# Five re-orderings in a two-block transformer kernel: first loads, one mean, block sums, a final scaling, and spatial gating in two halves

## The reference, cut to what matters

```python
# first block, x is [1, 1024, 1024]
h = rms_norm(x, mix_norm_g);  p = h @ w_in
y_a = spatial_gating(gelu(gm_u), gelu(gm_v), ...)   # layer norm of v, 4 causal 128x128 mixes, times u
y_b = conformer_conv(cv_a, cv_g, ...)               # 31-tap depthwise convolution, layer norm, silu
y_c = gated_deltanet(q, k, v, gate, beta, alpha, ...)
x = x + concat(y_a, y_b, y_c) @ w_out
h = rms_norm(x, ffn_norm_g)
x = x + (silu(h @ w_gate) * (h @ w_up)) @ w_down    # "ffn0"
x = rms_norm(x, final_norm_g)
# second block, 16 meta tokens put in front
x = x + 0.5 * swiglu(rms_norm(x, ...))              # "ffn1"
x = x + (attention and state-space branches) @ w_out_2   # "mix2"
x = x + 0.5 * swiglu(rms_norm(x, ...))              # "ffn2"
return rms_norm(x, final_norm_2)[:, 16:]
```

## Time and profile before

| | |
|---|---|
| median of 3 runs | 3499.8 us (3498.15 to 3500.18) |
| the profiled execution, its own time | 3500.61 us |
| its span, first to last instruction | 3498.8 us |
| PE busy | 3394.3 us, 97% |
| DVE, ACT, POOL busy | 1870.0, 1086.6, 1312.4 us |
| mean granted TensorE clock | 0.987 |
| the chain that ended last | nearly all PE |

### The profile page before, as it was taken

How to read it: one execution, slowest core, us unless ns; L and a number is a source line. 1 busy time by engine, 2 the same in 40 slices (tenths; PEclk the granted TensorE clock), 3 DMA queues, 4 the chain that set the end, 5 groups by cost and what they waited for, 6 DMA issues and landing times. The chain is left out here.

```text
span 3498.8 us, 52579 instructions
## 1 busy us (share of the span) xinstructions
PE 3394.3 (97%) x19644; PEld 2852.8 (82%) x19644; DVE 1870.0 (53%) x3044; ACT 1086.6 (31%) x1960; POOL 1312.4 (38%) x1559
## 2 busy tenths in 40 slices
PE   7999889999999999999999999999999999999998
PEld 5788778788888889899999878887778878888886
DVE  6966456766552263322221473846877476656324
ACT  5344533323321142111111243215664333332112
POOL 4433035455543352223322442311014545555334
PEclk9999899999999999999999999999999999999999
DMA  3112123332334321111111232101015333231543
GB/s 120 49 43 64 33 80 119 129 109 98 131 124 173 113 84 44 47 39 50 52 41 53 85 111 83 37 24 48 31 40 187 97 121 133 98 132 67 194 170 111
DMA packets 110227, 311.76 MB, mean 89 GB/s; under 512 B 21456, under 2 KB 24656, under 8 KB 109008
## 3 DMA queue, kind: packets, MB, share of 16 engines
q1 hardware_dynamic: 79344, 219.88, 19.5%
q10 hardware_dynamic: 30688, 89.22, 6.8%
HBM read 242.27 MB, written 65.73 MB: 88 GB/s over the span
## 5 line engine op out<-in xcount | busy, mean ns | idle before, releaser
L766 POOL TENSOR_TENSOR w_lo<-w_raw,w_hi 128x256 fp32r<-128x256 f32 (+4 forms) x1288 | 918.9, 745 | 1729.1 <-ACT w_hi L722 1728.8
L931 PE MATMUL acc<-h_hi,w_hi 128*128 128x512 f32 (+1 forms) x2576 | 927.3, 360 | 23.9 <-POOL w_lo L766 10.3
L932 PE MATMUL acc<-h_lo,w_hi 128*128 128x512 f32 (+1 forms) x2576 | 919.4, 357 | 0.0
L933 PE MATMUL acc<-h_hi,w_lo 128*128 128x512 f32 (+1 forms) x2576 | 918.4, 357 | 0.0
L931 PEld LDWEIGHTS acc<-h_hi,w_hi 128*128 128x128 f32 x2576 | 487.2, 189 | 99.0 <-issue 22.6
L932 PEld LDWEIGHTS acc<-h_lo,w_hi 128*128 128x128 f32 x2576 | 487.4, 189 | 69.5 <-issue 1.9
L933 PEld LDWEIGHTS acc<-h_hi,w_lo 128*128 128x128 f32 x2576 | 486.9, 189 | 69.8
L722 ACT CAST w_hi<-w_raw 128x1024 fp32r<-128x1024 f32 (+4 forms) x322 | 275.9, 858 | 831.4 <-PE acc L933 760.9
L749 POOL TENSOR_TENSOR w_lo<-w_sum,w_hi 128x512 fp32r<-128x512 f32 x180 | 264.5, 1474 | 276.1 <-ACT w_hi L1303 276.1
L931 PE MATMUL acc<-ff_hi,w_hi 128*128 128x512 f32 (+1 forms) x960 | 341.8, 356 | 8.5 <-POOL w_lo L766 3.9
L932 PE MATMUL acc<-ff_lo,w_hi 128*128 128x512 f32 (+1 forms) x960 | 337.7, 352 | 0.0
(11 more groups left out here) (435 smaller groups left out, 5172.8 us busy)
## 6 DMA issues: line engine op xcount, KB each, us to landing
w_raw<-in_w_in_dram SPq DMA_DIRECT2D x60, 512.0 KB, 3.6
w_raw<-in_ffn_w_dram SPq DMA_DIRECT2D x58, 512.0 KB, 3.6
ff_kept<-ff_hi SPq DMA_DIRECT2D x36, 512.0 KB, 7.6
ff_kept<-ff_lo SPq DMA_DIRECT2D x36, 512.0 KB, 8.3
w_raw<-in_ffn_w_dram SPq DMA_DIRECT2D x18, 1024.0 KB, 5.6
w_raw<-in_w_out_dram SPq DMA_DIRECT2D x32, 512.0 KB, 3.5
x<-x_kept ACTq DMA_DIRECT2D x6, 2080.0 KB, 8.1
w_raw<-in_w_gate_dram SPq DMA_DIRECT2D x9, 1024.0 KB, 6.3
```

Source lines behind the costliest of these rows:

```text
L766: pool.tensor_tensor(w_lo[:, j, a:a + step], w_raw[:, j, a:a + step], w_hi[:, j, a:a + step].bitcast(F32), ALU.subtract).then_inc(split_do ...
L931: pe.matmul(bank, wh, rh, start=(k == 0), stop=False)
L932: pe.matmul(bank, wh, rl, start=False, stop=False)
L933: ins = pe.matmul(bank, wl, rh, start=False, stop=(k == seg.kt - 1))
```

## The change

Five things are re-ordered. No arithmetic is added or dropped.

1. Start: parts 4 and 5 of x go from ACT's queue to SP's, behind a wait for part 1 and ahead of `consts`; `w_hi` of the first two slabs is made after the second and sixth row.
2. `pe_early`: the second half's mean is formed after four of the eight k of the first slab.
3. Sevens: the sums are formed in the order `FORMED`, with s6 and s7 ahead of s1 and s3; ACT's `high_sums` and DVE's `low_sums` move one e later, and `form_sums(2)`, `form_sums(3)` and `low_sums(2)` come to e = 4 and 5.
4. ffn1: the second half's 8 scalings leave `dve_fin` and go, two by two, ahead of the residuals of the four pairs of the first down projection.
5. Gating: events 0 and 1 at s = 2 and events 2 and 3 at s = 3, each behind that slab's key sums; the banks' order becomes dn0_0, gm_s0, gm_s1, dn1_0, gm_s2, gm_s3. The store of `gm_u` moves from ACT's s = 3 to s = 4.

```diff
+FORMED = ("s4", "s6", "s7", "s1", "s3")
...
-        for name in ["logits_0", ...] + [f"gm_t{e}" for e in range(4)] + [f"gm_s{e}" for e in range(4)]:
+        for name in ["logits_0", ...] + [f"gm_t{e}" for e in range(4)]:
             event(name)
-        for tile in range(12):
+        for name in ("dn0_0", "gm_s0", "gm_s1", "dn1_0", "gm_s2", "gm_s3"):
+            event(name)
+        for tile in range(2, 12):
...
                         load_x(sp, 2 * j)
                         load(0, j)
+                    sp.wait_ge(sem("x_full1"), 16)
+                    for g in (4, 5):
+                        load_x(sp, g)
                     sp.dma_start(consts[:, :], t["consts"]).then_inc(sem("consts_full"), 16)
...
-            for g in (1, 3, 4, 5):
+            for g in (1, 3):
                 load_x(act, g)
...
-                if k % 4 == 3:
+                if k % 4 == 1:
                     w_high(act, SEG["cv_first"], 0, k // 4)
...
             pe_ready(pe, name, 0)
-            pe_slab(pe, segs[0], 0, 0, h)
+            pe_slab(pe, segs[0], 0, 0, h, ks=range(KD // 2))
             pe_mean(pe, name, 1)
+            pe_slab(pe, segs[0], 0, 0, h, ks=range(KD // 2, KD))
             pe_slab(pe, segs[0], 0, 1, h)
...
-                if e in (2, 3):
-                    high_sums(e - 2)
+                if e in (3, 4):
+                    high_sums(e - 3)
...
-                for which in BLOCK_SUMS:
+                for which in FORMED:
...
                 plain(seg, i, c, f, e % 3)
-                if e in (2, 3):
+                if e >= 3:
+                    low_sums(e - 3)
+                if e >= 2:
                     form_sums(e - 2)
-                    low_sums(e - 2)
-                if e == 4:
-                    form_sums(2)
             own.wait()
             dve.sem_inc(ff_full, 1)
-            low_sums(2)
-            form_sums(3)
             low_sums(3)
...
-                if part < len(FQ) - 1:
+                if part == 0:
+                    for i in range(KD // 2):
+                        for j in range(2):
+                            fin_scale(dve, own, 1, 2 * i + j)
+                        own.wait()
+                        dve_residual_pair(dve, SEG[f"{name}_down0"], scale, i)
+                elif part < len(FQ) - 1:
                     dve_residual(dve, own, SEG[f"{name}_down{part}"], scale)
...
-                    for k in range(KD):
-                        own.mark(dve.scalar_tensor_tensor(x[:, k, cols], ...))
+                    for k in range(KD if half == 0 else 0):
+                        fin_scale(dve, own, half, k)
...
-                if s == GATING_AT:
-                    gating()
                 if 0 <= s - 2 < 12:
                     dn_event(s - 2)
+                if 0 <= s - GATING_AT < 2:
+                    gating(s - GATING_AT)
...
-                    if s - 1 == GATING_AT:
+                    if s - 1 == GATING_AT + 1:
                         act.wait_ge(sem("gm_gated"), 1)
...
-                if s == GATING_AT:
-                    gm_gating()
+                if 0 <= s - GATING_AT < 2:
+                    gm_gating(s - GATING_AT)
```

More of the change, by code:

```diff
@@ L480, in event @@
             EVENT[name] = (len(EVENT) % 2, len(EVENT) // 2)
-        for name in ["logits_0", "logits_1", "logits", "decays"] + [f"gm_t{e}" for e in range(4)] + [f"gm_s{e}" for e in range(4)]:
+        for name in ["logits_0", "logits_1", "logits", "decays"] + [f"gm_t{e}" for e in range(4)]:
             event(name)
-        for tile in range(12):
+        for name in ("dn0_0", "gm_s0", "gm_s1", "dn1_0", "gm_s2", "gm_s3"):
+            event(name)
+        for tile in range(2, 12):
             for c in range(2 if 4 <= tile < 8 else 1):
@@ L1284, in high_sum @@
                 _, _, _, (hi, _), total = block_sum(which, k)
-                act.wait_ge(later("s_sum"), later_count("s_sum", name, len(BLOCK_SUMS) * k + BLOCK_SUMS.index(which) + 1))
+                act.wait_ge(later("s_sum"), later_count("s_sum", name, len(FORMED) * k + FORMED.index(which) + 1))
                 act.copy(hi, total).then_inc(later("s_high"), 1)
@@ L1554, in dve_ffn, with dve_residual_pair @@
                     beside(seg.pairs - 1)
-                if part < len(FQ) - 1:
+                if part == 0:
[5 more added lines that the diff above has]
+                elif part < len(FQ) - 1:
                     dve_residual(dve, own, SEG[f"{name}_down{part}"], scale)
             own.wait()
+        def dve_residual_pair(dve, seg, scale, i):
+            for j in range(2):
+                for c, (c0, w) in enumerate(seg.chunks):
+                    acc_wait(dve, seg, i, j, c)
+                    xt = x[:, 2 * i + j, c0:c0 + w]
+                    dve.scalar_tensor_tensor(xt, acc[:, seg.bank(i, j, c), 0:w], scale, xt, ALU.mult, ALU.add).then_inc(acc_free[j], 1)
         def dve_residual(dve, own, seg, scale):
@@ L1656, in dve_fin, with fin_scale @@
                     own.link(dve.reciprocal(rs[:, cols], rs[:, cols]))
-                    for k in range(KD):
-                        own.mark(dve.scalar_tensor_tensor(x[:, k, cols], x[:, k, cols], param("final_g")[:, k:k + 1], rs[:, cols],
-                                                          ALU.mult, ALU.mult))
+                    for k in range(KD if half == 0 else 0):
+                        fin_scale(dve, own, half, k)
                 own.wait()
+        def fin_scale(dve, own, half, k):
+            cols = fin_columns(half)
+            own.mark(dve.scalar_tensor_tensor(x[:, k, cols], x[:, k, cols], param("final_g")[:, k:k + 1], rs[:, cols],
+                                              ALU.mult, ALU.mult))
         def flat(a, b):
@@ L1758, in gm_turn, with gating @@
                     aux_done(ins, f"gm_t{e}")
-            def gating():
+            def gating(half_tile):
                 pe.wait_ge(sem("gm_normed"), 1)
-                for e in range(4):
+                for e in (2 * half_tile, 2 * half_tile + 1):
                     ct, half = e // 2, e % 2
@@ L2317, in gm_norm, with gm_gating @@
                 dve.sem_inc(sem("gm_normed"), 1)
-            def gm_gating():
-                for e in range(4):
+            def gm_gating(half_tile):
+                for e in (2 * half_tile, 2 * half_tile + 1):
                     aux_wait(dve, f"gm_s{e}")
```

4 lines of the change are left out of this document (3 added, 1 removed).

## The result

The changed kernel takes 3479.0 us (median of 4 runs, 3474.2 to 3480.7), the kernel before 3499.0 beside it (4 runs). The ratio is 0.9941, 95% interval 0.9926 to 0.9956. So the change gains 20 us. The forecast was 34 us and 3466 us, with a range that ended at 3478.

A forecast was written before the change was run, and what follows sets the result against it. PE's own work was taken as the bound, leaving its 104.5 us of idle time and slow-clock matmuls to gain. Terms 12.7 + 12.4 + 4.8 + 2.8 + 1.4 = 34.1 us gave 3466 us, range 3458 to 3478.

The forecast's parts named there:

- gating in halves: Between slabs 2 and 4: PE's idle for gating banks and the low clock behind it go; 12.7 us.
- block sums: In ffn0 and ffn2: PE's 3.43 us idle for the last early pair's w_lo and low clock go; 12.4 us for both.
- ffn1's scaling: At ffn1's first down projection: banks freed sooner, PE's 3.12 us wait and low clock behind it go; 4.8 us.
- earlier mean: At the turn into mix2: second half's chain comes half a slab earlier, PE idles 3.5 instead of 6.28 us; 2.8 us.
- start: At the kernel's start: x lands earlier, PE begins 2.9 us earlier but keeps only 1.4 us.
- key sums at 1.84 us and two events, 4.13: Gating step: work left between slabs 2 and 3, priced at full speed, within the 12.7 us gain.
- Rival A: At the gating: the clock falls at the two new clusters, costing 3.4 to 6.7 us, 3471 us; chance 0.16.
- Next late: DVE's remaining sums ... at the first product: Block-sums step in ffn0/ffn2: DVE's sums, due before PE has done up0, are next late, within about 1 us.
- Rival B: In the sevens: the stall returns through POOL or late DVE sums, 3 to 6 us per stage, 3472 to 3478; chance 0.12.
- C: At the start: parts 4, 5 and consts queue up, consts late for the first mean by up to 8 us; chance 0.08.
- D: From 355 to 480: shifted phases leave small matmuls at 1.2 GHz, 3500 us and above; chance 0.03.
- E: Whole change: the edits do nothing, their waits being held by others, 3495 to 3500 us; chance 0.02.

The follow-up runs named there:

- e5: The changed kernel measured again with nothing altered, as base for later runs; 3478.8 us.
- e12: Changed kernel with gating halves mid-slab 3 and 4; in ffn0/ffn2 form_sums(2) later, three weight sums earlier, first two weight remainders on VectorE; 3473.6 us.
- e16: Changed kernel with its one-row gating bias matmuls made 128 rows deep, output unchanged; 3472.3 us.
- e1: Changed kernel with form_sums(2) behind the last early multiplication in ffn0 and ffn2; 3485.4 us.
- e14: e12 without VectorE's eight remainders of the s6 and s7 sums in ffn0 and ffn2; 3465.7 us.
- e6: e1 with the first two sums of weights ahead of the remainders of block sums 2 and 3; 3482.9 us.
- e3: Changed kernel with gating one event at a time: behind slabs 2 and 3 and in the middle of slabs 3 and 4; 3474.0 us.
- e8: e6 with the first two left operands' remainders on VectorE instead of POOL in ffn0 and ffn2, plus e3's gating at four places; 3475.8 us.
- e13: Kernel before with the start's edits alone (queue of first transfers, earlier first weight rounding); 3496.8 us.
- e2: Changed kernel with each gating half between the column halves of slabs 3 and 4; 3474.7 us.
- e15: Changed kernel without the gating's eight one-row bias matmuls (bias left out); 3469.8 us.
- e18: Changed kernel with e12's ffn0/ffn2 order, gating halves behind the key sums, bias added by VectorE instead of one-row matmuls; 3468.5 us.

## Why the prediction was wrong, step by step

| part | forecast | alone | by the traces |
|---|---|---|---|
| gating in halves | 12.7 | 6.0 | 6.4 |
| block sums | 12.4 | 4.3 | 3.2 |
| ffn1's scaling | 4.8 | 4.6 | 4.9 |
| earlier mean | 2.8 | 2.7 | 2.9 |
| start | 1.4 | 2.2 | 1.9 |
| sum | 34.1 | 19.8 | 19.3 |

The last column compares the first profile of the changed kernel with that of the kernel before; for the gating another profile gives up to 8.0 (46.4 - 38.4, e5).

**Gating: failed at "key sums at 1.84 us and two events, 4.13".** All its waits were right: PE has no idle time from 157 to 190, no bank was late, DVE's new wait cost nothing. What failed is the clock at which the events were priced: the forecast has them at full speed, and 13.9 us around them ran at half (10 to 14 in other profiles). With the clock held (e12's profile) the same matmuls give 46.4 - 34.0 = 12.4 us, the forecast's 12.7; with the halves at the slab's end it fell in all six profiles. Rival A had the effect and its price, 3.4 to 6.7 us for two clusters (measured 12.7 - 6.4 = 6.3), though not the depth as its cause. It was held at 0.16, because "each low stretch begins in or right after an idle stretch of PE of 3.12 us or more". That sentence was a pattern of the idle places, and the row that spoke against it was read and put aside: after the 4.10 us of idle the clock did not rise until the events were over the earlier trace rows. That the one-row matmuls of each event do it was in no step; `1*64` stands in the earlier trace rows.
The Trainium skill, TensorE: Matmul & The Clock Gate, "Part 1: The HAM clock gate", has a block that watches how busy PE is. In the changed kernel the profile counts PE busy for 33.00 of 33.00 us at a clock of 0.79, and e16 brings 1.00 with the same count of matmuls: a PE that the profile calls busy the whole time doesn't keep the clock up by that alone. Read as "no idle time, no fall", as the prediction read it, the rule was wrong here.

**Block sums: failed at "Next late: DVE's remaining sums ... at the first product".** The first half was right: the stall at 633 is gone, and ACT's `w_hi` comes in time. But the next consumer of DVE's order was not the first product; it was `pe_mixed`, 14 us earlier in the trace, whose bank is freed by the last early multiplication. That one stood behind `form_sums(2)` before the change too; the change put `low_sums(1)` in front of it as well, and PE came earlier, so that DVE's 3.24 us in hand became PE's 2.82 us of idle. The prediction walked DVE's queue to one deadline and did not ask what else stood in it. e1 to e14 say more: of the 4.5 us a stage the best order (e12) saves 1.3, and the rest is DVE's work as a whole. "I find both within about 1 us of each other" was the mis-sized comparison: PE waits 2.8 to 4.6 us a stage in the profiles from the changed kernel to e12. Rival B had the price (3 to 6 us a stage; measured 9.2 us in two) and, for e1, also the place; it was held at 0.12.
The Trainium skill, GPSIMD Engine Reference, "1. Specifications", says that POOL's SBUF interfaces are shared with VectorE, with contention where a VectorE instruction has two SBUF inputs. The traces agree: 6.71 us for two pieces and 2.99 us for two later ones (e1), 5.07 against 1.29 us for the same piece (e12, e14), and the other way round 5.89 against 3.70 us for VectorE's six (e6).

**ffn1's scaling: right**, mechanism and size; the clock is 1.00 in 1416 to 1428 and the idle is gone.

**Earlier mean: right in sum, off in its parts.** The turn into mix2 idles 4.05 us, not 3.5, and gives 2.0 us; 0.9 come from small gaps at ffn1's turn, whose waits the prediction passed over.

**Start: right**, a little low: PE's first matmul at 12.52 (forecast 13.2), the second mean waits 1.88 us instead of 0.71, and the first now waits 0.93 us as well.

**Rivals C, D and E** did not come: `consts` cost the first mean no 8 us (it waits 0.93 us, for DVE), the clock over 346 to 472 is 0.86 as before (0.86 over 355 to 480), and each edit did what it says. The range failed by 1 us because the two large steps share a blind spot (a stretch without idle time is priced at full clock, a queue is walked to one deadline) and were treated as if one could fail without the other.

## What to carry to other kernels

Where small matmuls are moved, read the granted clock beside the rows and the tile's depth in them; a bias added by a one-row matmul can cost more in clock than in time, and the same matmul padded to full depth cost no more time here (e16: 6.5 us for two lines). When an instruction is moved ahead of others on an engine, list every semaphore that those others signal, not only the last. One profile of a stretch isn't its price: read a second of the same kernel, above all where the clock moves (e3 and e8). When a wait vanishes and another of its size appears twice in a row, stop reordering and count the engine's work: take some of it away once (e14) before moving it again.

## What the runs showed of the hardware

- The TensorE clock went to half (0.79 over 33 us) with PE busy by the profile the whole time. With the eight bias matmuls (16 records) one row deep it fell in all six profiles where both halves stood behind the key sums (stretch 38.4 to 40.1 us), and in e13 with no key sums in front; with the same ones 128 rows deep it stayed at 1.00 (one profile; five timed runs within 2.4 us of each other, where the changed kernel's nine spread over 7.8). In the middle of slabs, one row deep, they brought 3.4 us of low clock (e2) or none (e12, e14).
- Key sums of one column, 128 rows deep, did not bring it down: in e15 and e18 they stand right before 2.0 us of gating matmuls, at a clock of 1.00.
- Two one-row matmuls of 512 columns (four records) took 1.01 us to the next group's start at full clock (e12), two of 128 rows 0.91 (e16): depth cost no time.
- Two POOL subtractions of 128x512 took 6.71 us beside VectorE's unbroken stream of subtractions and 2.99 us where that stream was looser (e1); one took 5.07 us beside it and 1.29 without it (e12, e14). With the roles reversed VectorE's six took 5.89 us (e6) instead of 3.70 (e1).
